# A mixture-of-experts stage whose chunks are done in an order of alternating expert groups, with row scatters that don't wait for one another

## The reference, cut to what matters

```python
aff = sigmoid(h @ w_router)                       # 16 experts in 4 groups of 4
score = aff + b_router
best = argmax over groups of (the two highest scores of the group, summed)
top_idx = top 2 of score inside group best        # both experts of a token lie in one group
top_w = aff[top_idx] / sum(aff[top_idx])
act = silu(h @ w_gate[e]) * (h @ w_up[e]) * combine[e]
out = sum over e of act @ w_down[e]
x = layer_norm(alpha * x + out)
```

## Time and profile before

| | us |
|---|---|
| runs, median of 3 | 1550.72 |
| runs, lowest and highest | 1549.3, 1556.68 |
| profiled execution, span from first to last instruction | 1557.7 |
| TensorE busy in it | 1435.5 (92%) |
| expert part of layer 1, of layer 2 (about) | 560 to 760, 1336 to 1527 |

### The profile page before, as it was taken

The page is one execution under the profiler, slowest core; times in us unless marked ns, Lnnn a source line. Parts: engine busy times, 40 slices in busy tenths (PEclk is TensorE's granted clock), DMA queues, the critical chain, the costliest instruction groups (busy, mean ns, idle before and its releaser), DMA issues. The chain is left out here.

```text
span 1557.7 us, 23011 instructions
## 1 busy us (share of the span) xinstructions
PE 1435.5 (92%) x9168; PEld 1169.0 (75%) x9168; DVE 801.4 (51%) x1351; ACT 612.7 (39%) x1156; POOL 173.0 (11%) x152
## 2 busy tenths in 40 slices
PE   7999899999999969989499999999999999699886
PEld 6897566999997747656378966669999977476553
DVE  3224767433334777566542266664333346775566
ACT  3322568322221236555224325773222212366550
POOL 3011000000000112223012210000000001123221
PEclk9999999999999879999699997999999998799998
DMA  8234401222223659997324143012222246599963
GB/s 277 77 123 158 142 2 33 85 84 92 72 78 149 250 207 347 353 312 236 105 85 142 55 171 129 1 47 83 72 92 77 74 167 227 211 343 354 310 206 129
DMA packets 55861, 239.75 MB, mean 154 GB/s; under 512 B 11718, under 2 KB 19796, under 8 KB 45964
## 3 DMA queue, kind: packets, MB, share of 16 engines
q1 hardware_dynamic: 44716, 216.08, 38.7%
q0 software_dynamic: 11040, 22.21, 6.1%
HBM read 224.55 MB, written 34.49 MB: 166 GB/s over the span
## 5 line engine op out<-in xcount | busy, mean ns | idle before, releaser
L1435 PE MATMUL ps<-xT_high,w_high 128*128 128x288 f32 x704 | 208.0, 295 | 0.0
L1436 PE MATMUL ps<-xT_low,w_high 128*128 128x288 f32 x704 | 207.2, 294 | 0.0
L1437 PE MATMUL ps<-xT_high,w_ring_low 128*128 128x288 f32 x704 | 206.3, 293 | 0.0
L1533 ACT ACTIVATE tanh_gate<-ps 128x576 f32<-128x576 f32 x48 | 31.3, 652 | 295.0 <-PE ps L1437 295.0
L1437 PEld LDWEIGHTS ps<-xT_high,w_ring_low 128*128 128x128 f32 x704 | 132.6, 188 | 0.0
L1436 PEld LDWEIGHTS ps<-xT_low,w_high 128*128 128x128 f32 x704 | 132.5, 188 | 0.0
L1435 PEld LDWEIGHTS ps<-xT_high,w_high 128*128 128x128 f32 x704 | 132.1, 188 | 0.0
L1852 PE MATMUL ps<-down,hidT 128*128 128x512 f32 x256 | 117.3, 601 | 4.4 <-ACT hidT L1903 2.4
L1327 POOL TENSOR_TENSOR ln_rs<-ln_mv,const 128x1 f32<-128x1 f32 (+1 forms) x20 | 17.5, 874 | 879.7 <-DVE ln_mv L1322 879.7
L1585 DVE SCALAR_TENSOR_TENSOR branch_part<-tanh_gate,ps 128x576 f32<-128x576 f32 x32 | 24.1, 754 | 175.7 <-ACT tanh_gate L1533 175.7
L557 PE MATMUL ps<-z_w_high_part,oT_low 128*128 128x454 f32 x260 | 96.8, 372 | 8.5 <-DVE z_w_ring_low L1041 8.5
(11 more groups left out here) (368 smaller groups left out, 3333.4 us busy)
## 6 DMA issues: line engine op xcount, KB each, us to landing
gate_up<-in_we SPq DMA_DIRECT2D x34, 2048.0 KB, 12.6
down<-in_we SPq DMA_DIRECT2D x32, 1024.0 KB, 10.4
w_ring<-in_wm SPq DMA_DIRECT2D x28, 640.0 KB, 4.1
z_w_ring<-in_wtm SPq DMA_DIRECT2D x30, 454.0 KB, 4.1
w_ring<-in_wm SPq DMA_DIRECT2D x16, 768.0 KB, 4.5
w<-in_w SPq DMA_DIRECT2D x2, 2048.0 KB, 9.4
sel_pages<-in_sel_pages SPq DMA_DIRECT2D x32, 128.0 KB, 2.0
win_rows<-in_win_rows SPq DMA_DIRECT2D x2, 2048.0 KB, 7.9
```

The lines of the kernel that those rows point to most:

```text
L1435: pe.matmul(out, w[0], x[0], start=first, stop=False)
L1436: pe.matmul(out, w[0], x[1], start=False, stop=False)
L1437: return pe.matmul(out, w[1], x[0], start=False, stop=last)
```

## The change

The static chunks are done in the order `TURNS`: the n-th turn works on expert `TURNS[n]`. Turns 0 to 11 take the three first groups in rotation, one expert each; turns 12 to 15 stay as they are. All that belongs to an expert follows: the gate, up and down loads, the two slot columns of gather and scatter, and the column of combine weights. Buffers, sides and semaphores still go by the turn number. Neighbouring static turns up to the 13th belong to different groups, so their scatters share no row. POOL's wait on `y_stored` before a static scatter is gone; ACT's wait before it overwrites `y[side]`, and the waits in the loop, are as before.

```diff
             for n in range(RING_E):
-                sp.dma_start(k.gu[:, n, :], io["we"][l, n, :, 0:4096]).then_inc(k.gu_in[n], 16)
+                sp.dma_start(k.gu[:, n, :], io["we"][l, TURNS[n], :, 0:4096]).then_inc(k.gu_in[n], 16)
...
+TURNS = (0, 4, 8, 1, 5, 9, 2, 6, 10, 3, 7, 11, 12, 13, 14, 15)
+assert sorted(TURNS) == list(range(E)) and TURNS[STATIC - 2:] == tuple(range(STATIC - 2, E))
+assert all(a // 4 != b // 4 for a, b in zip(TURNS, TURNS[1:STATIC - 1]))
...
                 for n in range(RING_E):
-                    load_dw(fixed_chunk(n), n)
+                    load_dw(fixed_chunk(n), TURNS[n])
...
                     sp.wait_ge(gu_done, n - RING_E + 1)
-                    load_gu(fixed_chunk(n), n)
+                    load_gu(fixed_chunk(n), TURNS[n])
                     if n > RING_E:
                         sp.wait_ge(dn_done, n - RING_E)
-                        load_dw(fixed_chunk(n - 1), n - 1)
+                        load_dw(fixed_chunk(n - 1), TURNS[n - 1])
...
+                def slots(which, n):
+                    at = TURNS[n] if n < STATIC else n
+                    return table[:, which, at:at + 1]
...
                     pool.wait_ge(xt_done, n + 3)
-                    gather(n % 2, table[:, 0, n + 4:n + 5])
+                    gather(n % 2, slots(0, n + 4))
                     pool.wait_ge(y_out, n + 1)
-                    if n:
-
-                        pool.wait_ge(y_stored[(n - 1) % 2], 16 * ((n + 1) // 2))
-                    scatter(n % 2, table[:, 1, n:n + 1])
+
+                    scatter(n % 2, slots(1, n))
...
                     rows_low(n + 2)
-                    hidden(fixed_chunk(n), wslot[:, n:n + 1])
+                    hidden(fixed_chunk(n), wslot[:, TURNS[n]:TURNS[n] + 1])
```

More of the change, by code:

```diff
@@ L1971, in looked_up @@
                     return dst[:, 0:1]
+                def slots(which, n):
+                    at = TURNS[n] if n < STATIC else n
+                    return table[:, which, at:at + 1]
                 for n in range(2):
-                    gather(n, table[:, 0, n:n + 1])
+                    gather(n, slots(0, n))
                 for n in range(2):
                     pool.wait_ge(xt_done, n + 1)
-                    gather(n, table[:, 0, n + 2:n + 3])
+                    gather(n, slots(0, n + 2))
                 pool.wait_ge(table_ready, 2)
@@ L1982, in _ @@
                     pool.wait_ge(xt_done, n + 3)
-                    gather(n % 2, table[:, 0, n + 4:n + 5])
+                    gather(n % 2, slots(0, n + 4))
                     pool.wait_ge(y_out, n + 1)
-                    if n:
-                        pool.wait_ge(y_stored[(n - 1) % 2], 16 * ((n + 1) // 2))
-                    scatter(n % 2, table[:, 1, n:n + 1])
+                    scatter(n % 2, slots(1, n))
                 pool.wait_ge(xt_done, STATIC + 1)
-                gather(0, table[:, 0, STATIC + 2:STATIC + 3])
+                gather(0, slots(0, STATIC + 2))
                 with pool.Fori(0, pairs(pool)) as p:
```

## The result

| | before | with the change |
|---|---|---|
| median of the runs, us | 1549.32 (10 runs) | 1541.80 (10 runs) |
| lowest and highest, us | 1547.56, 1558.88 | 1535.04, 1548.45 |
| ratio to the kernel before | | 0.9932, 95% interval 0.9914 to 0.9951 |
| span of the profiled execution, us | 1557.7 | 1540.3 |

The change makes the kernel faster, by 7.5 us between the medians and by 10.5 us by the ratio (interval 7.6 to 13.3). The prediction was 1526 us with a range of 1517 to 1540; the time lies 1.8 us beyond the range, and less than half of the forecast 24.1 us came. Of the 17.4 us between the two spans some 7 lie outside the experts' stages. A span is 1.7 us shorter than the time of the same execution (1540.3 and 1541.97 with the change), so the profiled execution of before, 1557.7 us of span, was itself some 10 us over its median.

The account below looks back on a forecast made before the run. It took GpSimd's chain of one-at-a-time scatters, which made gathers late, as the bound. Its terms, 20.8 - 4 + 6 + 1.3 = 24.1 us off 1550.7, gave 1526 us, with a range of 1517 to 1540.

Parts of the forecast that it names:

- What bounds the kernel now: Expert stages: one-at-a-time scatters turn in 11.64 us where TensorE wants 10.13, so gathers are late; weights are not waited for.
- Step (1): Order of the experts: the same blocks and bytes in another sequence, at no cost.
- Step (2): Expert stages: dropping GpSimd's wait on the neighbour's scatter wins TensorE's excess over its own period, 20.8 us together.
- Step (3): Weight loads and DMA engines after the change: 369 GB/s asked, 350 moved; 2 us a layer kept back, -4 us.
- ScalarE's cover: ScalarE's wait before it overwrites `y`: 20.3 us of room for a scatter's landing of 11.2, so no cost.
- rival D: GpSimd's removed wait is replaced by ScalarE's on the same landings, transfers still one by one: about 1550 us, chance 0.04.
- Step (4): Ends of the layers: earlier scatters let `x` be read back sooner, 6 us in layer 1 and 1.3 in layer 2.
- B: DMA engines already full: the stall moves from rows to weights, only the layers' ends gain; 1543 us, chance 0.12.
- C: More scatter traffic beside the weights pulls the rate down from chunk 3 on, to 319 GB/s: 1561 us, chance 0.06.
- A: Software queue's own pace of 11.64 us per scatter and gather: gathers late again though issued early; 1533 us, chance 0.16.
- a sign of its failure: Expert stages: scatters in flight together landing much later than 11 us would show the forecast wrong.

Follow-up runs that it names:

- `order_only`: The change with GpSimd's wait for the neighbour's scatter put back, so only the order of the experts is new: 1555.71 us, ratio 1.0008 to the kernel before.
- `new_plain`: The change with the expert scatters writing their rows instead of adding them: 1521.92 us, ratio 0.9785 to the kernel before.
- `new_empty`: The change with the expert scatters' slots put out of range, so that they move no row: 1523.86 us, ratio 0.9809 to the kernel before.
- `split_load`: The change with each gate_up load cut into two halves, the first issued some 2.8 us earlier: 1543.04 us, ratio 0.9934 to the kernel before.

## Why the prediction was wrong, point by point

*What bounds the kernel now*: half right. The chain of one-at-a-time scatters, 11.64 us a turn, was what made gathers late, and it is gone. But beside it stood a second bound that was nearly as long. With the DMA engines at 0.95 to 0.97 in the earlier trace rows, "weights are not what TensorE waits for" held only because TensorE's stalls for rows gave the weights time: their landings grew to 14.1 us (loads of 640 to 660 us) and fell to 11.1 (680 to 700) as the stalls came.

*Step (1), the order costs nothing*: right, `order_only` has 1.0008.

*Step (2), the excess of 20.8 us*: the amount is right. `new_plain` and `new_empty` take 81.1 us for the eight periods in both layers, and the kernels with less traffic show that 29 us can be had in all. What failed is that the step took the excess as belonging to the wait. One reading in it is the wrong way round: the gather doesn't go "some 10 us after the chain would have let it go" but sooner, 0.8 us after `rows_t` has emptied its buffer (chunk 12 of layer 1) where it was 7.5.

*Step (3), what is late next*: this is the step that failed. It worked out 369 GB/s as asked for and 350 as moved, which was the right comparison, and then kept back only 2 us a layer, since the weights had 1.0 to 2.7 us of room and scatters would "give back what they lag". The room was read from landings of 12.9 us under the old chain, as if a landing were a constant; with the change it grows by 1.3 us a chunk, to 20.6, against the 15.6 that were there. The room was a stock that five or six chunks used up. The shortfall over the floor is 87.08 - 81.04 = 6.0 us in layer 1 and 6.8 in layer 2, 12.8 in place of 4: a term mis-sized by 8.8 us. It also took a scatter's bytes for its cost. A scatter of 0.30 MB that adds takes the engines' time of 0.6 MB of weights (1.56 / 2.63), so a chunk is nearer to 4.0 MB than to 3.74. And the 350 GB/s come from a stretch in which the backlog was growing: TensorE ran free in it on weights asked for 15.6 us ahead.

*Step (3), ScalarE's cover*: a landing of 11.2 us against 20.3 of room "costs nothing until a landing takes twice its median". It came to 19 us in the median and 20.7 at most, and ScalarE waited 2.7 + 2.7 us for it in layer 1. This lay beside the wait for weights, so rival D holds in this small part only.

*Step (4), the ends*: 6 + 1.3 us forecast, 1.4 + 1.0 measured, mis-sized by 4.9 us. The sum took two links of 12.2 us; the first took 19 (700.96 to 720.1), so scatter 13 went out at 731.58, some 6 us before TensorE's end and not 11, and `x` was read 3.6 us after that end. That SP's order holds up the next weights was seen rightly ("at most 7.0 us"), but the gain was made to hang on the scatters; moving two loads brings it, and more. Where the scatters did land after 11 us, in `split_load`, the wait of 18.99 us fell to 13.54: 5.5 of the forecast 6 us came, so this step failed with its landings alone.

*The rivals.* B named the outcome, "the stall moves from the rows to the weights", and its sign in the trace, ScalarE's conversion waiting for `gate_up`; its price, 1543 us, is 1.2 us off, but by luck: it took all of its 7.3 us from the ends and nothing from the stages, where the traces have 2.4 and 8.0. It had 0.12. Against it stood that 8% of rate were to be had in the late half. It was 6% (342 over 324), and a chunk with its addition needed more than that. C did not come: the change's windows stay over the 331 GB/s from which it decides. A did not come either: no gather that was issued in time was waited for, though one took 20.5 us to land (680 to 700 us).

The forecast named a sign of its failure, scatters in flight together that land much later than 11 us. The sign came, but it was not the cause: `split_load` has the same time with scatters that land after 10.8 us. The cause had a price part of which could have been worked out from the earlier trace rows alone: 3.74 MB / 350 GB/s = 10.7 us a chunk, which leaves 0.55 x 8 = 4.4 us a layer and not 2, before any price of the addition.

## What to carry to other kernels

Where the DMA engines are over 0.95 busy in a stage, a wait that is taken away saves only what the engines' time leaves: add up that time for one turn of the loop, kind by kind, and set it beside the period that is hoped for, before costing the wait. The sum is rough (0.7 us low here), so look at the landings of like loads one after the other as well: if they grow while the consumer still runs free, more is asked for than comes, and the room between issue and use is a stock that lasts for some turns. A median over the stretch hides that. And look at what an in-order queue of loads has put behind a late wait: at the end of a stage that was worth more here than the change.

## What the runs showed of the hardware

An indirect scatter that adds to DRAM took 1.56 us of the 16 engines' time for 0.30 MB (up to 1.8 in other traces), one that writes the same rows 0.71 us. That alone moved the kernel by some 23 us (ratio 0.9932 to 0.9785; 20 between the medians). With the adding scatters the weights' landings grew from 9.1 to 20.6 us within one stage, with the plain ones they stayed at 11.2 or below. On that the Trainium skill, "DMA: Bandwidth & Descriptors", section Rules for kernel authors, says that an accumulate reads its destination and writes it later, which agrees with an addition being dearer, though it gives no price.
